# V's weighted sum in two column halves: gathered rows on the left, a dense product on the right

## What is computed

```python
eidx = e1 * PEER_NKEYS + e2            # e1, e2: 0..127, chosen by two top-16 lists
gates = jax.nn.softmax(vs, axis=-1)
def block(args):                        # 128 tokens, kk = 8 * 16 = 128 choices each
    xb, ib, gb = args
    act = jax.nn.gelu(jnp.einsum('tkd,td->tk', expert_u[ib], xb))
    return jnp.einsum('tk,tkd->td', act * gb, expert_v[ib])
...
h = h + peer(rms_norm(h, ffn_norm_gain[i]), ...)
gate = jax.nn.sigmoid(rms_norm(h, ple_norm_gain[i]) @ w_ple_gate[i])
h = h + gate * (p[i] @ w_ple_proj[i])
```

## Time and profile before

| | us |
|---|---|
| median of three executions | 2516.05 |
| the profiled execution | 2524.99 |
| its span, first to last instruction | 2523.6 |

### The profile page before, as it was taken

One profiled execution on the slowest core, in us unless ns is written; L12 is line 12 of the kernel. 1 busy time (PEld: TensorE's weight loads), 2 busy tenths in 40 slices (PEclk: granted clock), 3 DMA queues, 4 the chain that ended last, 5 costly groups with the idle time before them and its releaser, 6 DMA issues.

```text
span 2523.6 us, 19173 instructions
## 1 busy us (share of the span) xinstructions
PE 2126.6 (84%) x7436; PEld 1353.1 (54%) x7436; DVE 1411.3 (56%) x1775; ACT 644.1 (26%) x868; POOL 653.2 (26%) x522
## 2 busy tenths in 40 slices
PE   8999985878777877777777777778999999999999
PEld 6876874433222432222222222225888778888887
DVE  4567568546666776545444444445554565654454
ACT  4444432101110110000000000003443353543342
POOL 0000004345445555454454444430000000000000
PEclk9999986889999999999999999999999999999999
DMA  7442539889999999999999999994555544455543
GB/s 274 150 150 93 179 132 381 331 316 410 421 421 421 421 422 421 421 421 422 421 421 422 422 422 422 421 396 193 200 190 193 176 156 176 168 189 194 200 175 142
DMA packets 105354, 751.20 MB, mean 298 GB/s; under 512 B 11952, under 2 KB 11952, under 8 KB 14384
## 3 DMA queue, kind: packets, MB, share of 16 engines
q0 software_dynamic: 73728, 536.90, 51.5%
q1 hardware_dynamic: 29376, 207.63, 23.3%
q10 hardware_dynamic: 2160, 5.45, 0.6%
HBM read 747.84 MB, written 2.10 MB: 297 GB/s over the span
## 4 chain that ended last, share of the span: by engine, by line
PE 40%; DMA 35%; DVE 5%; POOL 2%; issue 2%; ACT 1%; DVEq 0%; ACTq 0%; POOLq 0%
PE ps L324 29%; DMA xT_rows<-in_expert_v,idx 25%; PE ps L597 9%; DMA raw<-in_expert_u,idx 4%; DMA W<-in_expert_u,idx 2%; DMA raw<-in_expert_v,idx 1%; POOL xT_rows L287 1%; DMA W<-in_expert_v,idx 1%; DMA xT_rows<-in_expert_u,idx 1%; POOL W L287 1%; DVE raw L1528 1%; DVE wlo L1161 1%; PE ps L345 1%; DVE xT_rows L1528 1%; DVE W L1528 1%
## 5 line engine op out<-in xcount | busy, mean ns | idle before, releaser
L324 PE MATMUL ps<-whi,xT 128*128 128x512 f32 x2800 | 676.7, 394 | 12.8 <-ACT whi L764 10.0
L1161 DVE TENSOR_TENSOR wlo<-raw,whi 128x2048 fp32r<-128x2048 f32 x195 | 445.5, 2288 | 289.4 <-ACT whi L764 285.8
L324 PEld LDWEIGHTS ps<-whi,xT 128*128 128x128 f32 x2800 | 526.4, 189 | 128.7 <-issue 11.1
L597 PE MATMUL ps<-xT_rows,W 128*128 128x512 f32 x936 | 435.7, 608 | 151.2 <-DMA xT_rows<-in_expert_v,idx 150.1
L764 ACT ACTIVATE whi<-raw 128x2048 fp32r<-128x2048 f32 x195 | 372.4, 1914 | 449.0 <-PE ps L324 275.3
L1528 DVE CUSTOM_DVE_ANT_0 xT_rows<-xT_rows,W 128x2048 f32<-128x2048 f32 x112 | 256.4, 2292 | 250.8 <-DMA xT_rows<-in_expert_u,idx 250.5
L597 PEld LDWEIGHTS ps<-xT_rows,W 128*128 128x128 f32 x936 | 170.0, 191 | 414.2 <-issue 308.5
L324 PE MATMUL ps<-wlo,xT 128*128 128x512 f32 x1400 | 350.5, 393 | 10.6 <-DVE wlo L1161 10.6
L597 PE MATMUL ps<-W 128*128 128x512 f32 x536 | 255.1, 619 | 85.4 <-DMA W<-in_expert_v,idx 61.7
L597 PE MATMUL ps<-raw,W 128*128 128x512 f32 x512 | 244.9, 623 | 81.2 <-DMA raw<-in_expert_v,idx 81.2
L324 PEld LDWEIGHTS ps<-wlo,xT 128*128 128x128 f32 x1400 | 264.6, 189 | 68.0 <-DVE wlo L1161 13.0
(11 more groups left out here) (253 smaller groups left out, 1244.4 us busy)
## 6 DMA issues: line engine op xcount, KB each, us to landing
raw<-in_weights SPq DMA_DIRECT2D x196, 1024.0 KB, 4.9
h<-in_x SPq DMA_DIRECT2D x8, 256.0 KB, 6.8
out<-h ACTq DMA_DIRECT2D x8, 256.0 KB, 2.7
xT_rows<-in_expert_v,idx POOLq DMA_INDIRECT x122, 15.8
xT_rows<-in_expert_u,idx POOLq DMA_INDIRECT x112
W<-in_expert_u,idx POOLq DMA_INDIRECT x72
raw<-in_expert_u,idx POOLq DMA_INDIRECT x72, 10.8
W<-in_expert_v,idx POOLq DMA_INDIRECT x70
```

Source lines behind the costliest of these rows:

```text
L324: return pe.matmul(ps[:, (banks_of(b) if bank is None else bank) + t, 0:cols_n], x[:, q0 + qn * 4 + k, s], w_[:, cs], start=start, stop=stop)
L597: m = pe.matmul(ps[:, (4 if t == 0 else 0) + b, :], diag[:, i % DIAGS, :], slots[SLOT_OF[n]][:, b * NC:(b + 1) * NC], start=(unit % NH == ...
L1161: v.tensor_tensor(lo, raw[:, RAW_OF[c], :], hi.bitcast(F32), ALU.subtract).then_inc(sem["lo_done"], 1)
```

## The change

`expert_v` is stored as two arrays, the left and the right 1024 columns.

Left half: one gather brings 128 rows of 4 KB (0.5 MB). The V rows of units 0 to 10 (176) go through diagonals on PE, two banks each, mixed into the order of the U rows from unit 1 on. The left rows of units 11 to 15 (80) come after the last U row and are added by VectorE, one `scalar_tensor_tensor` of 1024 columns each.

Right half: the 16384 x 1024 array is read whole, in 128 blocks of 128 experts by 1024 columns, by SyncE. The weights of a token are laid out as a table of 128 x 128 (e1 by e2). To build it, PE turns the lists of e1, e2 and weights so that choices lie on partitions; per token VectorE writes a one-hot matrix of e1 times the weight, ScalarE one of e2 (|e2 - i|, then 1 minus that, cut at 0), and PE multiplies the two. Four tokens make a batch; ScalarE copies it out of PSUM into `wts`, with a stride of 128 elements. The 32 batches of t = 0 go beside units 8 to 12, the 32 of t = 1 beside rows 2 to 15 of unit 15; in these VectorE also writes the e2 side of each third batch. The 16 choices of unit 15 for t = 1 come too late for the table: they are 16 further gathered half rows ("right") that VectorE adds.

The dense loop splits each block and each pair of table columns into high and low parts, and makes 12 matmuls of 512 columns per block. The 96 added rows go beside it on VectorE. p's projection is computed behind it, with its chunks split near the loop's end.

The slots become rings laid over other buffers: three U and two V slots at first, then eight and eight, eight and six from unit 8, three for the U rows of unit 15, four for the added rows. The lists of e1 and e2 are kept (`picks`). The core of the diff:

```diff
...
+V_ON_PE = 11
+LATE = UNITS - 1
+BLOCKS = 128
+BATCH = 4
...
+def row_order():
+    order, v, total = [], 0, 16 * V_ON_PE
+    for n in range(16 * UNITS):
+        order.append(("u", n // 16, n % 16))
+        while n >= 16 and v < total and v * 16 * (UNITS - 2) < total * (n - 15) and v // 16 < n // 16:
+            order.append(("v", v // 16, v % 16))
+            v += 1
+    order += [("left", unit, j) for unit in range(V_ON_PE, UNITS) for j in range(16)]
+    return order + [("right", LATE, j) for j in range(16)]
+
+
+ROW_ORDER = row_order()
...
+RAW_0, WHI_0, WLO_0, XT_0, W_0 = 0, 8192, 12288, 16384, 28672
+EARLY_U, EARLY_V = (W_0 + 8192, W_0 + 10240, 4096), (6144, 7168)
+MID_U = (W_0 + 8192, W_0 + 10240, 4096, 0, XT_0, XT_0 + 2048, XT_0 + 4096, XT_0 + 6144)
+MID_V = (6144, 7168, 2048, 3072, WHI_0, WHI_0 + 1024, WHI_0 + 2048, WHI_0 + 3072)
+LATER_U, LATER_V = tuple(range(0, 16384, 2048)), tuple(range(XT_0, XT_0 + 6144, 1024))
+LAST_U = (XT_0, XT_0 + 2048, XT_0 + 4096)
+ADDED = (XT_0 + 4096, XT_0 + 5120, W_0 + 3072, W_0 + 1024)
...
+TABLES_AT = {("u", NH, 6): 0, ("u", LATE, 1): 1}
+BATCHES_AT = {}
+for _i in range(32):
+    BATCHES_AT.setdefault(("u", NH + (8 + 2 * _i) // 16, (8 + 2 * _i) % 16), []).append(_i)
+    BATCHES_AT.setdefault(("u", LATE, 2 + 14 * _i // 32), []).append(32 + _i)
...
-TWO_RAW = range(C_PQ + 6, C_GATE + 2)
+TWO_RAW = range(C_PQ + 6, C_PROJ)
...
+        block_raw = (W[:, 0:HALF], tmp[:, :], W[:, 2048:3072])
+        block_hi, block_lo = over("block_hi", xT_at, 0, [2, HALF]), over("block_lo", xT_at, 2048, [2, HALF])
+        wt_hi, wt_lo = over("wt_hi", xT_at, 6144, [2, NT, 256]), over("wt_lo", xT_at, 7168, [2, NT, 256])
...
+            sp.wait_ge(sem["v_used"], 16 * V_ON_PE)
+            sp.wait_ge(sem["idx1_ok"], NH)
+            for b in range(BLOCKS):
+                if b == 2:
+                    sp.wait_ge(sem["u_used"], 16 * UNITS)
+                if b >= 3:
+                    sp.wait_ge(sem["dense_lo"], b - 2)
+                sp.dma_start(block_raw[b % 3], v_right[128 * b:128 * b + 128, :]).then_inc(block_in[b % 3], 16)
+                if b in (20, 36, 52, 68):
+                    sp.wait_ge(sem["dense_used"], b - 4)
+                    load_chunk({20: C_GATE, 36: C_GATE + 1, 52: C_PROJ, 68: C_PROJ + 1}[b])
+            for c in range(C_GATE + 2, CHUNKS):
+                load_chunk(c)
...
+                if (kind, unit, j) == ADDED_ROWS[2]:
+                    g.wait_ge(sem["u_used"], 16 * UNITS)
+                if (kind, unit, j) == ADDED_ROWS[3]:
+                    g.wait_ge(sem["built"], 64)
+                gather(n, {"u": expert_u, "v": v_left, "left": v_left, "right": v_right}[kind], unit // NH, 16 * (unit % NH) + j)
...
             def proj_step(c):
-                    pe.wait_ge(sem["query_out"], 8)
-                    pe.wait_ge(evac_of(B_PQ + 3)[0], evac_of(B_PQ + 3)[1])
...
+                    if c == 0:
+                        pe.wait_ge(sem["peer_in"], 6 + 2 * n)
...
+            def build_weights(i):
+                n = 128 if i < 32 else 16 * (LATE - NH)
+                if i < 32 or i % 3 != 2:
+                    pe.wait_ge(sem["one2_a"], sum(k < 32 or k % 3 != 2 for k in range(i + 1)))
+                else:
+                    pe.wait_ge(sem["one2_v"], sum(k >= 32 and k % 3 == 2 for k in range(i + 1)))
+                pe.wait_ge(sem["one1_v"], i + 1)
+                if i >= 2:
+                    pe.wait_ge(sem["wt_out"], i - 1)
+                for k in range(BATCH):
+                    m = pe.matmul(ps[:, 2 + i % 2, k * 128:(k + 1) * 128], one2[0:n, i % 2, k, :], one1[0:n, i % 2, k, :], start=True, stop=True)
+                m.then_inc(sem["built"], 1)
...
+                    for b in range(2):
+                        m = pe.matmul(ps[:, (4 if unit < NH else 6) + b, :], diag_of(i), slots[n][:, b * NC:(b + 1) * NC],
+                                      start=(unit % NH == 0 and j == 0), stop=(i in (127, 16 * V_ON_PE - 1)))
...
+            pe.wait_ge(sem["wt_out"], 64)
+            for b in range(BLOCKS):
+                def product(t, n, w_, v_, start, stop):
+                    return pe.matmul(ps[:, 2 * n + t, :], w_[:, b // 2 % 2, t, b % 2 * 128:b % 2 * 128 + 128], v_[:, b % 2, n * NC:(n + 1) * NC],
+                                     start=start, stop=stop)
+
+                if b % 2 == 0:
+                    pe.wait_ge(sem["wt_lo"], b // 2 + 1)
+                pe.wait_ge(sem["dense_hi"], b + 1)
+                for t in range(NT):
+                    for n in range(2):
+                        product(t, n, wt_hi, block_hi, b == 0, False)
+                        product(t, n, wt_lo, block_hi, False, False)
+                pe.wait_ge(sem["dense_lo"], b + 1)
+                for n in range(2):
+                    for t in range(NT):
+                        m = product(t, n, wt_hi, block_lo, False, b == BLOCKS - 1)
+                m.then_inc(sem["dense_used"], 1)
+
+            pe.wait_ge(sem["peer_in"], 4)
+            pe.wait_ge(sem["added"], len(ADDED_ROWS))
             entry(E_PLE, 0)
-            pe.wait_ge(sem["peer_in"], 8)
             entry(E_PLE, 1)
+            proj_step(0)
+            entry(E_PLE, 2)
+            proj_step(1)
...
+            def one_hot(i):
+                n, t = (128, 0) if i < 32 else (16 * (LATE - NH), 1)
+                if i == 0 or i == 32:
+                    a.wait_ge(sem["tabs_out"], t + 1)
+                if i >= 2:
+                    a.wait_ge(sem["built"], i - 1)
+                at = one2[0:n, i % 2, :, :]
+                for k in range(BATCH):
+                    c = i % 32 * BATCH + k
+                    m = a.activation(at[:, k, :], iota[0:n, :], ACT.Abs, bias=tables[0:n, t, 1, c:c + 1], scale=-1.0)
+                m.then_inc(sem["ones_a"], 1)
+                ones[0] += 1
+                a.wait_ge(sem["ones_a"], ones[0])
+                a.activation(at, at, ACT.Relu, bias=st[0:n, 94:95], scale=-1.0).then_inc(sem["one2_a"], 1)
+
+            def weights_out(i):
+                t, c = i // 32, i % 32 * BATCH
+                a.wait_ge(sem["built"], i + 1)
+                a.activation(wts[t][:, :, c:c + BATCH].rearrange("p e n -> p n e"),
+                             ps[:, 2 + i % 2, :].rearrange("p (n e) -> p n e", n=BATCH), ACT.Copy).then_inc(sem["wt_out"], 1)
...
+            a.wait_ge(sem["dense_used"], BLOCKS)
+            entry(E_PLE, 0, C_PROJ)
+            entry(E_PLE, 1, C_PROJ)
+            split(C_GATE)
+            proj_out(0)
+            entry(E_PLE, 2, C_PROJ)
+            split(C_GATE + 1)
+            proj_out(1)
...
+            def one_hot(i):
+                n, t = (128, 0) if i < 32 else (16 * (LATE - NH), 1)
+                if i == 0 or i == 32:
+                    v.wait_ge(sem["tabs_out"], t + 1)
+                if i >= 2:
+                    v.wait_ge(sem["built"], i - 1)
+                for k in range(BATCH):
+                    c = i % 32 * BATCH + k
+                    m = v.tensor_scalar(one1[0:n, i % 2, k, :], iota[0:n, :], tables[0:n, t, 0, c:c + 1], tables[0:n, t, 2, c:c + 1],
+                                        ALU.is_equal, ALU.mult)
+                m.then_inc(sem["one1_v"], 1)
+                if i >= 32 and i % 3 == 2:
+                    for k in range(BATCH):
+                        c = i % 32 * BATCH + k
+                        m = v.tensor_scalar(one2[0:n, i % 2, k, :], iota[0:n, :], tables[0:n, t, 1, c:c + 1], None, ALU.is_equal)
+                    m.then_inc(sem["one2_v"], 1)
...
+                v.scalar_tensor_tensor(h[:, 1, cs], slots[n][:, :], act[:, 1, c:c + 1], h[:, 1, cs], ALU.mult, ALU.add).then_inc(sem["added"], 1)
...
+            rows_done = 0
+            for b in range(BLOCKS):
+                v.wait_ge(sem["dense_hi"], b + 1)
+                if b >= 2:
+                    v.wait_ge(sem["dense_used"], b - 1)
+                v.tensor_tensor(block_lo[:, b % 2, :], block_raw[b % 3], block_hi[:, b % 2, :].bitcast(F32), ALU.subtract).then_inc(sem["dense_lo"], 1)
+                if b % 2 and b + 1 < BLOCKS:
+                    wt_split((b + 1) // 2)
+                if b == 4:
+                    unit_weights(LATE)
+                if b == 52:
+                    v.wait_ge(sem["pT_hi"], 1)
+                    v.tensor_tensor(pTl[:, :, :], pTs, pTh[:, :, :].bitcast(F32), ALU.subtract).then_inc(sem["pT_lo"], 1)
+                if b == 120:
+                    v.wait_ge(sem["dense_used"], 112)
+                    split(C_PROJ)
+                while rows_done < len(ADDED_ROWS) and rows_done * 120 < len(ADDED_ROWS) * (b - 2):
+                    added_row(rows_done)
+                    rows_done += 1
+            v.wait_ge(sem["dense_used"], BLOCKS)
+            for n in range(2):
+                for t in range(NT):
+                    cs = slice(HALF + n * NC, HALF + (n + 1) * NC)
+                    if n == 0 and t == 1:
```

(6 more changed lines are left out.)

## The result

| | before | after |
|---|---|---|
| median of four executions, us | 2518.71 | 2555.78 |
| profiled execution, us | 2524.99 | 2556.88 |
| its span, us | 2523.6 | 2555.4 |

The ratio is 1.0145, with a 95% interval of 1.0131 to 1.0160. The forecast was 2531, 12 to 15 us more than before; the measured loss is 37 us. The sign was right and the time lies in the range, but the size was not.

The account below looks back on a forecast made before the run. Bytes were taken to bound the gather units, at 421 GB/s. Stage terms summed to a span of 2538.4 us; plus 1.4 and less 8.9 gave 2531, with 2505 to 2560 for the likeliest case and 2462 to 2605 overall.

Parts of the forecast that it names:

- Units 0 and 1: First two gather units: 64 us with three U slots in place of four, and 88 us (75 to 95).
- Units 2 to 7: Early gather units: 60 us for unit 2, 58 each for 3 to 7, bytes and VectorE both nearly full; 350 us.
- Units 8 to 14: Later gather units: byte rate kept by sixteen slots queuing 12 MB, table work hidden; seven units at 56, 392 us.
- GpSimd: Gather issue: 28.6 gathers per unit, about one passing at each end of a dot, one per 1.24 us elsewhere.
- Rival B: Gather units: GpSimd locked out by running dots, about 0.35 us per row, +73, total 2604; chance 0.12.
- Unit 15: Last gather unit: 8 us dry queue, then table batches between dots at 5.2 us per row; 86 us (70 to 105).
- the dry wait: Start of unit 15: its first gather waits for the last V row's use, queue runs dry, 8 us.
- Product: Dense loop: 128 blocks at 2.85 us, TensorE's own 2.72, plus 5 to start; 370 us, bounds 350 and 420.
- Rival C: Dense product: the ring of three block buffers sets the pace, 3.23 us per block, 414 us, total about 2580; chance 0.15.
- Hand-over: From product to gate's first chunk: two projection steps and splits no longer hidden under gathers; 19 us (14 to 25).
- Profile against median: Whole time: 8.9 us subtracted because the earlier profiled execution lay that far above its median.
- Rival A: Whole kernel: stages mesh, units 2 to 14 at the byte rate, product 354, total 2463, faster; chance 0.33.

Follow-up runs that it names:

- slots in turn: Changed kernel with the same row slots in another order, so no row takes over a just-filled slot at ring changes (units 8 and 15): 2537.6 us, ratio 1.0067.
- the three cures together: Changed kernel plus four block buffers, reordered row slots, and ScalarE's copy in runs of four with a new one-hot split: 2518.9 us, ratio 0.9997.
- a run that took 27 us away: Changed kernel with V rows behind the 48th row loaded by SyncE as plain DMAs from fixed places instead of GpSimd gathers: 2528.7 us, ratio 1.0047.
- half dots: Changed kernel with each dot in units 8 to 14 run over 1024 of its 2048 columns: 2544.0 us, ratio 1.0097.
- eleven and ten units: Units of V's left half on TensorE, in the changed kernel with four block buffers, reordered slots, new copy and one-hot split: 2518.9 and 2515.7 us.

## Why the prediction was right in sign and wrong in size

The mechanism was the forecast's: fewer bytes in the units, paid back behind them in unit 15, the product and the hand-over. Point by point:

- *Units 0 and 1* (64 and 88; 60.1 and 83.3): right within 5 us, both a little too dear.
- *Units 2 to 7* (350; 346.7): right. VectorE is 95% busy in units 4 to 7 and its heads' choice hides, as said; these four took 56.1 each, a little under the 57 to 60 forecast for them, and units 2 and 3 61.2.
- *Units 8 to 14* (392; 410.6). This is the step that failed: "seven units at 56", resting on the sentence that sixteen slots keep 12 MB queued. From unit 8 on there are fourteen, 11 MB, and they keep it queued only inside a ring. At the change of rings one row takes over the slot of a row four places before it, and I read the order of the rings only for unit 15. The runs show in its place a gather queue that stands still for 12.85 us and DMA engines that are dry for 8. Of the 18.6 us, 5.9 lie in unit 8, 8.6 in units 9 to 13, and 4.1 in unit 14, where the wait fell that the sum had put into unit 15. The kernel with its slots in turn takes 391.6, 19.0 less.
- *GpSimd* (28.6 gathers per unit; one meeting each dot): the count was right, and I drew no price from it. This is the other part of the same step, a wait put at nothing. 28.6 x (1.70 + 0.30) = 57.2 against 55.5 by bytes; five units measured 57.7 each. Rival B priced this at 73 us by letting each wait breed more; nothing of that kind happened.
- *Unit 15* (86; the dry wait of 4.1 that fell into unit 14, and 93.9, so 98.0). The dry wait was half of my 8, and 12 are missing in all. The batches were too cheap: VectorE 1.11 per four one-hot rows in place of 0.65, ScalarE's copy 1.05 in place of 0.6. TensorE's small products had no term of their own and make 25.7% of the chain, at a granted clock of 0.60, and the product's first matmul comes 10.7 us after the last dot. No run gives each of these its part of the 12.
- *Product* (370; 373.3): right, TensorE at 351 and 22 lost to landings, where I had allowed 22. Rival C's 414 needed the ring of blocks to set the pace throughout; ScalarE waited for 57 of the 128 blocks, 1.8 us each.
- *Hand-over* (19; 20.8) and *tail*: right.
- *Profile against median*: 8.9 subtracted, 1.1 found. One profiled execution's distance from its median is luck of that execution and should have stood in the range, not in the sum.
- Rival A (2463) is ruled out for this kernel: with the three cures together eleven units still give 2518.9.

## What to carry to other kernels

A ring that hides latency has to be checked where it changes, not where it turns: for each row, count how many places back in the queue lies the row whose use it waits for, and look for the smallest number. A queue in order pays for one such row with everything behind it. When a cure moves the total as a theory says, cut the time into the stretches that the theory names before believing it: a run that took 27 us away looked like proof of one cause, and it had cured two at once. Windows pointed to the other, though work that moves across their borders can mislead; only an edit for each cause by itself (half dots, slots in turn) parted them.

## What the runs showed of the hardware

- A write of ScalarE that puts each 4-byte element 512 bytes from the last took 1052 ns for 512 elements; the same elements written in runs of four took 589, though then the reads from PSUM are the ones that stride. The Trainium skill ("SBUF — State Buffer", Specifications (TRN2)) gives 16-byte cachelines that want at least two hits each; the trace agrees, four floats being one such line.
- A VectorE tensor_scalar of 128 elements per partition with per-partition operands took 341 ns (median of 256), and four of them in a row 1.11 us together; the 64-wide one in the earlier trace rows took 196.
- A gather that meets a dot ended 0.81 us after it; in each of units 8 to 14 of the changed kernel 14 to 16 gathers took over 2 us so. Their mean went from 1.70 to 1.0 us with the dots halved. The Trainium skill ("SBUF — State Buffer", Who interferes with whom) says that GpSimd's reads block behind a VectorE instruction with two SBUF inputs; this trace agrees. The runs show that it costs time here only where GpSimd's own issue is the bound: before, gathers met dots too and the DMA engines moved 421 GB/s.
- With three block buffers the product took 363 to 373 us in the profiles of kernels that left it alone; with four 351.7 to 352.4 (eleven and ten units). Why the first scatter so is open.
